# The w_down loads of a mixture-of-experts layer issued from GpSimd's queue, all others from SyncE's

## The reference, cut to what matters

```python
def clamped_swiglu(hu):
    x_glu = jnp.minimum(hu[..., ::2], SWIGLU_LIMIT)
    x_lin = jnp.clip(hu[..., 1::2], -SWIGLU_LIMIT, SWIGLU_LIMIT)
    return x_glu * jax.nn.sigmoid(SWIGLU_ALPHA * x_glu) * (x_lin + 1.0)

def expert_chunk(args):
    toks, e = args
    hu = x_pad[toks] @ w_up[e] + b_up[e]
    return clamped_swiglu(hu) @ w_down[e] + b_down[e]
```

## Time and profile before

| | |
|---|---|
| median of 3 runs | 1337.93 us (1336.80 to 1339.74) |
| the profiled execution | 1338.13 us, of which the span from first to last instruction is 1336.2 us |
| PE busy | 1157.8 us, 87% of the span |
| DVE, ACT busy | 312.0 us and 258.3 us |
| POOL busy | 0.2 us, 4 instructions |
| moved by DMA | 464.89 MB, mean 348 GB/s |
| SyncE's queue (q1) | 100112 packets, 460.47 MB |
| ScalarE's queue (q10) | 2374 packets, 3.84 MB |
| the chain that ended last | PE 59%, DMA 26%, SPq 8%, DVE 4%, issue 3% |

### The profile page before, as it was taken

How to read it: one execution, slowest core, us unless ns; L and a number is a source line. 1 busy time by engine, 2 the same in 40 slices (tenths; PEclk the granted TensorE clock), 3 DMA queues, 4 the chain that set the end, 5 groups by cost and what they waited for, 6 DMA issues and landing times.

```text
span 1336.2 us, 21387 instructions
## 1 busy us (share of the span) xinstructions
PE 1157.8 (87%) x7951; PEld 575.0 (43%) x7952; DVE 312.0 (23%) x802; ACT 258.3 (19%) x395; POOL 0.2 (0%) x4
## 2 busy tenths in 40 slices
PE   5999899987989769988998988989988788788795
PEld 4745588744344324434343343342443233433233
DVE  2025445274111110202211121211111112111112
ACT  2135422123021111001112021111121111111112
POOL 0000000000000000000000000000000000000000
PEclk8899999997999898999999999999999989899898
DMA  9942565453789999549999999999999999999996
GB/s 356 380 168 94 200 243 218 161 228 148 290 342 416 418 417 418 215 164 420 416 418 417 419 414 417 417 419 418 417 418 419 417 417 417 417 418 418 419 417 271
DMA packets 102526, 464.89 MB, mean 348 GB/s; under 512 B 8188, under 2 KB 9556, under 8 KB 69590
## 3 DMA queue, kind: packets, MB, share of 16 engines
q1 hardware_dynamic: 100112, 460.47, 86.0%
q10 hardware_dynamic: 2374, 3.84, 0.8%
HBM read 463.24 MB, written 1.05 MB: 347 GB/s over the span
## 4 chain that ended last, share of the span: by engine, by line
PE 59%; DMA 26%; SPq 8%; DVE 4%; issue 3%; ACT 0%; DVEq 0%; ACTq 0%
PE psum L974 17%; DMA ring<-in_w_up 17%; PE psum L599 16%; PE psum L1047 9%; DMA ring<-in_w_down 8%; PE psum L908 5%; SPq L557 4%; SPq L552 3%; PE psum L966 3%; PE psum L1065 2%; PE psum L668 2%; DMA ring<-in_ada_w 1%; PE psum L605 1%; DVE area L1744 1%; PE psum L949 1%
## 5 line engine op out<-in xcount | busy, mean ns | idle before, releaser
L974 PE MATMUL psum<-ring,area 128*32 128x512 f32 (+2 forms) x2432 | 395.3, 627 | 45.2 <-DMA ring<-in_w_up 44.9
L974 PEld LDWEIGHTS psum<-ring,area 128*32 128x32 f32 (+2 forms) x2432 | 105.2, 122 | 329.4 <-issue 248.4
L1047 PE MATMUL psum<-ring,area 128*32 128x256 f32 (+2 forms) x2080 | 199.4, 422 | 30.1 <-DMA ring<-in_w_down 15.3
L908 PEld LDWEIGHTS psum<-area 128*128 128x128 f32 x1056 | 128.6, 202 | 31.1 <-issue 31.1
L908 PE MATMUL psum<-area 128*128 128x128 f32 x1056 | 135.2, 289 | 0.3 <-DVE area L1635 0.3
L1047 PEld LDWEIGHTS psum<-ring,area 128*32 128x32 f32 (+2 forms) x2080 | 71.8, 115 | 147.2 <-issue 79.6
L1704 DVE TENSOR_SCALAR area<-psum 128x256 f32<-128x256 f32 x51 | 21.7, 425 | 386.4 <-PE psum L974 386.4
L1257 ACT ACT_TABLE_LOAD x32 | 41.1, 1283 | 355.3 <-PE psum L949 355.3
L1269 ACT ACTIVATE area<-area 128x256 f32<-128x256 f32 x51 | 21.3, 417 | 400.0 <-DVE area L1704 400.0
L599 PE MATMUL psum<-ring,hT 128*128 128x512 f32 (+1 forms) x192 | 77.5, 559 | 0.0
L599 PE MATMUL psum<-hT,ring 128*128 128x256 f32 x320 | 71.1, 381 | 0.0
(11 more groups left out here) (201 smaller groups left out, 671.1 us busy)
## 6 DMA issues: line engine op xcount, KB each, us to landing
ring<-in_w_up SPq DMA_DIRECT2D x256, 1024.0 KB, 18.9
ring<-in_w_down SPq DMA_DIRECT2D x128, 1024.0 KB, 22.0
ring<-in_ada_w SPq DMA_DIRECT2D x12, 2048.0 KB, 16.4
ring<-in_w_in SPq DMA_DIRECT2D x10, 2048.0 KB, 13.2
ring<-in_w_out SPq DMA_DIRECT2D x2, 2048.0 KB, 10.2
ring<-in_w_in SPq DMA_DIRECT2D x3, 1024.0 KB, 15.7
ring<-in_w_branch_b SPq DMA_DIRECT2D x1, 2048.0 KB, 9.5
cst<-in_cst ACTq DMA_DIRECT2D x1, 1184.5 KB, 8.0
```

Of the source, the lines that this page charges most:

```text
L908: ins = pe.matmul(ps[banks[i]][:, kk % 4 * P:(kk % 4 + 1) * P], h2[:, tt, kk * P:(kk + 1) * P], S[:, tt, 0:P], start=(tt == 0 and kk % 4 = ...
L974: ins = pe.matmul(ps[b][g * P // G:(g + 1) * P // G, 0:w], XT[:, kk, t0:t0 + P // G], wt[:, c0:c0 + w], start=False, stop=kk == KT - 1, sk ...
L1047: ins = pe.matmul(ps[b][g * M:(g + 1) * M, 0:w], hidT[:, p, q * P + of * M:q * P + (of + 1) * M], down_weights(kk)[:, g * W + d * CW:g * W ...
```

## The change

The function `down_load` and the three places that call it move, unchanged, from SyncE's stream to GpSimd's. The destinations, the sources, the semaphores that are waited for and those that are raised are the same. GpSimd now reads the expert's number from `order_i` for itself. SyncE's loop holds only the `up_load`s. So there are two streams that issue, and neither waits for the other.

```diff
             for kk in range(KT):
                 if kk % 2 == 0:
                     sp.wait_ge(*released[names[NF + kk // 2 - RING]])
                 up_load(0, kk)
-            for j in range(FT // 2):
-                if j % 2 == 0:
-                    sp.wait_ge(*released[names[NF + 4 + j // 2 - RING]])
-                down_load(0, j)
             sp.wait_ge(order_ready, 1)
             with sp.Fori(1, E) as e:
...
                     up_load(number, kk)
-                for j in range(FT // 2):
-                    if j < FT // 2 - 1:
-                        sp.wait_ge(dn_used, (FT // 2 - 1) * e - (FT // 2 - 1) + j + 1)
-                    else:
-                        sp.wait_ge(dn_full, MAX_D * e)
-                    down_load(number, j)
...
+        @block.gpsimd
+        def _(gp):
+            def down_load(e, j):
+                to = slot(NF + 4 + j // 2)[:, j % 2 * 2 * D:(j % 2 + 1) * 2 * D].rearrange("p (k n) -> p k n", k=2)
+                src = a["w_down"][0][ds(e, 1), j * 2 * P:(j + 1) * 2 * P, :]
+                gp.dma_start(to, src.rearrange("e (k p) n -> p (e k) n", p=P)).then_inc(dn_tile[j], 16)
+
+            for j in range(FT // 2):
+                if j % 2 == 0:
+                    gp.wait_ge(*released[names[NF + 4 + j // 2 - RING]])
+                down_load(0, j)
+            gp.wait_ge(order_ready, 1)
+            with gp.Fori(1, E) as e:
+                number = expert_at(gp, e)
+                for j in range(FT // 2):
+                    if j < FT // 2 - 1:
+                        gp.wait_ge(dn_used, (FT // 2 - 1) * e - (FT // 2 - 1) + j + 1)
+                    else:
+                        gp.wait_ge(dn_full, MAX_D * e)
+                    down_load(number, j)
```

More of the change, by code:

```diff
@@ L552, in up_load @@
                 sp.dma_start(up_weights(kk), src.rearrange("e p n -> p (e n)")).then_inc(up_tile[kk], 16)
[L554 to L557, removed]
             for kk in range(KT):
```

## The result

The changed kernel takes 1403.05 us (median of 4 runs, 1402.48 to 1404.68). The kernel before, run beside it, takes 1337.37 us. The ratio is 1.0488, with a 95% interval of 1.0471 to 1.0504: slower by 65.7 us. The profiled execution has a span of 1402.9 us.

A forecast was written before the change was run, and what follows sets the result against it. PE bounds the largest expert's stretch, DMA from 601 us to the end, both in large turns. Late down loads add 39.0 + 5.8 + 9.8 = 54.6, less 4.6: +50 us on 1338.1, 1388 us; range 1348 to 1410.

The forecast's parts named there:

- The mechanism: Two queues alternate packet by packet; 4 KB down rows beside 8 KB up rows land late: 1388 us, chance 0.50.
- freeing SyncE: SyncE no longer issues 128 down loads; claimed to gain nothing, its issuing being hidden behind a queue of some 20 us.
- The first rival: Down gets half of the bytes or more, so up tiles come late: about +30 us, 1368 us, chance 0.30.
- The slow queue: GpSimd's issue or a share below one third makes a round longer than 30.0 us: 1410 us and above, chance 0.08.
- the faster rate: Two queues keep the engines fuller where DMA limits, a rate higher by 4.5%: about 1319 us, chance 0.08.
- middle turns: Stretches of a middle and two small experts: PE has 15 us to spare, so they stay 90 us.
- The four large turns: Stretches of a large and two small experts: PE and DMA both full, 92 us each rising to about 100.
- The round: A set of four down loads, sharing with up loads, takes 4 x 2.55 + 8 x 2.48 = 30.0 us from issue.
- the four places before large experts: Last down load needed 19.41 to 21.08 us after release; 30.0 instead costs 10.4, 9.1, 10.6, 8.9: 39.0 us.
- The one before the largest expert: The set before that expert has 24.20 us; 30.0 instead costs 5.8 us, which nothing makes up for.
- what is given back: 4.6 us taken off the sum, because the up queue need not be full for the whole of each round.
- the first case: Engines alternate packet by packet, so down gets one byte to up's two: 1388 us, own range 1365 to 1405, chance 0.50.

The follow-up runs named there:

- e3: Changed kernel with w_down's rows taken in pairs, one 8 KB run per partition, so both queues' packets are of one size: 1358.56 us, 1.0129 to before.
- e7: Changed kernel with each up tile loaded as two halves, so packets are 4 KB on both queues: 1399.06 us, 1.0434 to before.
- e8: Changed kernel with up tiles in halves (4 KB packets) and w_down in 8 KB runs, so down gets two thirds: 1400.12 us, 1.0456 to before.
- e1: Kernel before with every expert load, w_up's and w_down's, issued by GpSimd in the same order, one queue: 1337.48 us, 0.9997 to before.
- e2: Changed kernel with issuers swapped, w_up's loads by GpSimd and w_down's by SyncE: 1401.25 us, 1.0469 to before.
- e6: Kernel before, one queue, with each up tile loaded as two halves of 1024 columns, so all packets are 4 KB: 1358.57 us, 1.0157 to before.
- e4: Kernel before, one queue, with w_down's rows taken in pairs, one 8 KB run per partition: 1329.98 us, 0.9940 to before.

## Why the prediction was right, and where its sizes were off

**The mechanism held.** No gain came from freeing SyncE. GpSimd's queue got as many packets as SyncE's, as the row on SyncE's and ScalarE's queues had let expect: 755 to 752. The first rival (down gets half or more) has the opposite mark, waits for w_up, and is not what happened here; e3, e7 and e8 made it happen. The slow queue is ruled out as the cause by e1 and e2, and the faster rate by the slices, 416 to 419 GB/s where full.

The Trainium skill's rule of turns of 9 to 17 descriptors ("DMA: Bandwidth & Descriptors", "Queues, rings and completion order") would have given another share if the two queues bundled differently; e3, with rows of one size, shows 145 to 145, so they do not. Whether a turn is one record or a bundle these counts do not tell, since equal bundles give the same counts. The prediction read more out of the earlier trace rows than 1248 to 1236 shows when it called that the finer step; the share of bytes, on which its sum rests, is the same either way.

**Signs that came out otherwise.** The prediction wanted down loads to land about 30 us after issue and up tiles as before. The medians are 18.1 and 13.6 us, where they were 22.0 and 18.9. It had taken the time of a whole set for that of each load: the four of a set share the queue and land one after the other, and only the last of a set takes 31 us. "Down lands in under 20 us" was to be a mark of the first rival, and it stands in this trace beside waits for w_down, so it does not tell the two apart. The prediction also called itself wrong if the middle turns got shorter than 90 us, since then the rate would have changed. They took 85.5, 88.9 and 93.1 us, in place of 90.4 each, and the rate in each of them is 418 GB/s, as before. So that sign was badly chosen: a turn of PE can be shorter at the same rate, when loads ran ahead while PE was waiting.

**Where it costs.** The four large turns grew by 56 us, as forecast from PE's slack. In the middle turns PE waited for w_down too, 29.7 us in place of 6.0, but for w_up only 7.9 in place of 27.4, and the three together got no longer (267 us in place of 271).

**The round.** I had 30.0 us for a set of four, from its issue. In the set of the second chain line the first load is issued at 721.47 us and the last at 724.05. GpSimd's queue moves its first packets only at about 725.4 us (none before 725, 16 from 725 to 726), and the last load lands at 755.76. So the sharing takes 30.4 us, as forecast, and what the 30.0 left out are the 4 us from the first issue to the first packet. Counted from the last issue, as in the chain, that is 31.71. It is hardly a matter of GpSimd's issuing: in e2, where SyncE issues the down loads, the five lines at the same places have 31.65, 31.55, 30.51, 31.37 and 31.38 us. Against the earlier trace rows the four places before large experts (610.93, 700.02, 791.82, 880.54) grew by 12.6, 10.8, 11.7 and 10.7 us in place of 10.4, 9.1, 10.6 and 8.9. The one before the largest expert grew from 24.20 to 29.86 us, 5.7 in place of 5.8.

**The term that I did not have: TensorE's clock.** The four large turns grew by 14 us each. Of the 13.4 us of the first, 10.8 lie in the round (31.71 against 20.87) and the rest behind it, up to the next large expert. The timeline of PE in the changed kernel there:

```profile
755.80 1.93 PE L1054 MATMUL psum<-ring,area 128*32 128x256 f32 x16 [5.27 <-DMA ring<-in_w_down]
758.28 2.09 PE L1072 MATMUL psum<-area 32*128 32x256 f32 x16 [0.54 <-DVE area L1751]
...
762.11 5.37 PE L973 MATMUL psum<-bup,yaT 128*64 128x512 f32 x16
```

The down group takes 1.93 us where it took 1.07, though it is the same work. In the table of stretches (PE busy, PEld, DVE, ACT, POOL, clock, DMA share, GB/s):

```profile
700.00:726.00 26.00, 22.26 (x240) 11.54 (x237) 5.46 (x14) 4.56 (x6) 3.90 (x6) 1.00 0.86 343
742.00:768.00 26.00, 13.34 (x84) 4.39 (x74) 1.98 (x6) 3.16 (x3) 2.85 (x4) 0.61 1.02 416
```

From 700 to 726 us the granted clock is 1.00 of 2.4 GHz. From 742 to 768, with waits of 6.15 and 5.27 us in it, it is 0.61: most of that stretch ran at the lower level, 1.2 GHz. From the end of the last down group to the start of the next L981 it takes 9.7 us (757.73 to 767.41), and before it took 8.4 (722.00 to 730.43). With the 0.9 us of the group itself that is 2.1 of the 2.6 us. That PE's waits bring the lower clock with them is what these rows show side by side; no run here changes the clock alone.

The Trainium skill treats this in "TensorE: Matmul & The Clock Gate", section "Part 1: The HAM clock gate": TensorE runs at the lower of two clocks after it has been idle and returns to the full one when it has been kept at work. The trace agrees, with 0.61 in that stretch.

**The term that I had too small: what is given back.** I took off 4.6 us. The last two columns of the table give 4 and 7, 11 us in all. In the middle turns and behind them PE catches up: up tiles are ahead there, as the waits for w_up in the middle turns indicate, 7.9 us in place of 27.4.

**The sum, as forecast and as measured**, by the table's stretches. To the largest expert 5.8 and 6. Largest and two small 10.4 and 15. Four large turns, the last of which ends at the first middle expert, 9.1 + 10.6 + 8.9 + 9.8 = 38.4 and 57. Given back 4.6 and 11. Together 50 and 67. So the term that was mis-sized is "with 30.0 in place of them": it should have been 31 to 32, with some 3 us more in each large turn for the work behind it, of which 2.1 us in the first turn lie where the granted clock was lower; the rest is not explained. The losses were set 23 us too low in all and what is given back 7 us too low; that these partly cancel is luck. 1403 lies near the upper end of the first case's own range, 1365 to 1405.

One slip changes only a bound: a set issued at 669.27 that takes 30.0 us ends at 699.3 and not at 700.3.

## What to carry to other kernels

Where a ring of buffers is just as large as one round of work and loads limit the kernel, a single queue in the order of use is worth keeping: here a second queue moved no more bytes and gave up the order. If two queues must share, look at the size of the packets, since the queues got equal numbers of them: the stream with 4 KB rows beside one with 8 KB rows got a third. And look for the stretches in which the consumer has no slack; there lateness cost most here (56 us in the four large turns), and there the work behind the waits ran at a lower granted clock as well.

## What the runs showed of the hardware that I had not expected

The rate depends on the packets' size also in a single queue: 408 to 411 GB/s in the full slices with 4 KB alone (e6), 414 to 420 with 4 and 8 KB mixed, 420 to 424 with 8 KB alone (e4, but for one slice of 412). e6 also has twice as many transfers for w_up; e4 has as many as before. That was 20.7 us and 8 us of the whole, and e4's edit, one run of 8 KB per partition, is the only one here that made the kernel faster.

GpSimd's transfers, of which I had no row, run at the same rate as SyncE's (e1), and its stream spends little on them:

```profile
L578 POOL DMA_DIRECT2D ring<-in_w_down x128 | 91.7, 716 | 1281.6 <-PE psum L1054 958.5
```

716 ns for one, 91.7 us for all 128.
